# Moving the joining factors of the first head group into the gather loop, and starting GpSimd's decay arguments before them

## The reference, cut to what matters

```
S_t = diag(exp(log_g_t)) S_{t-1} + k_t^T v_t,     o_t = q_t S_t
```

## Time and profile before

| what | value |
|---|---|
| median of 3 runs | 2969.95 us (2969.85 to 2975.12) |
| profiled execution: its own time | 2969.85 us |
| profiled execution: span from first to last instruction | 2968.1 us |
| busy: PE, DVE, ACT, POOL | 82%, 71%, 38%, 28% of the span |
| `phase_scan` of layer 0 | about 206 to 344 us |
| `phase_scan` of layer 1 | about 2039 to 2128 us |

### The profile page before, as it was taken

The page is one execution under the profiler, slowest core; times in us unless marked ns, Lnnn a source line. Parts: engine busy times, 40 slices in busy tenths (PEclk is TensorE's granted clock), DMA queues, the critical chain, the costliest instruction groups (busy, mean ns, idle before and its releaser), DMA issues. The chain is left out here.

```text
span 2968.1 us, 36810 instructions
## 1 busy us (share of the span) xinstructions
PE 2424.4 (82%) x13114; PEld 1822.0 (61%) x13114; DVE 2110.2 (71%) x4654; ACT 1124.8 (38%) x2650; POOL 840.8 (28%) x688
## 2 busy tenths in 40 slices
PE   5979799896659888888888888688797897777776
PEld 3779565674659777777777777478556542223222
DVE  3567763499949888888888888667653898745444
ACT  3433354336633333333333333342344433334332
POOL 1004001230004434343433434103004453433431
PEclk8995799998889999999999999797798999999999
DMA  5210205264379999999999999221103999999997
GB/s 213 89 32 2 96 4 188 77 235 165 142 297 400 419 419 420 420 419 419 419 420 420 418 416 407 101 82 33 39 1 131 420 421 421 421 421 422 422 422 300
DMA packets 147671, 817.13 MB, mean 275 GB/s; under 512 B 16200, under 2 KB 17800, under 8 KB 64672
## 3 DMA queue, kind: packets, MB, share of 16 engines
q0 software_dynamic: 73728, 536.90, 43.7%
q1 hardware_dynamic: 73760, 277.87, 24.2%
HBM read 796.89 MB, written 17.83 MB: 274 GB/s over the span
## 5 line engine op out<-in xcount | busy, mean ns | idle before, releaser
L2412 POOL DMA_INDIRECT pair_ring<-in_uv_first,eid x256 | 395.0, 1543 | 780.9 <-DVE pair_sum L2555 274.5
L2051 PE MATMUL ps<-pair_ring,pair_diag 128*128 128x512 f32 x1024 | 475.4, 609 | 143.5 <-ACT pair_diag L2130 139.4
L2436 PE MATMUL ps<-peer_h,peer_uv 128*128 128x256 f32 x2048 | 474.8, 386 | 40.4 <-DMA peer_uv<-in_uv_dense 40.4
L2262 DVE CUSTOM_DVE_ANT_0 pair_ring<-pair_ring,hT 128x1024 f32<-128x1024 f32 x256 | 312.9, 1222 | 208.7 <-DMA pair_ring<-in_uv_rows,eid 208.6
L2051 PEld LDWEIGHTS ps<-pair_ring,pair_diag 128*128 128x128 f32 x1024 | 187.1, 192 | 421.0 <-ACT pair_diag L2130 222.6
L2436 PEld LDWEIGHTS ps<-peer_h,peer_uv 128*128 128x128 f32 x2048 | 387.3, 194 | 94.2 <-DMA peer_uv<-in_uv_dense 30.6
L119 PE MATMUL ps<-h_both 128*128 128x256 f32 x1024 | 316.0, 309 | 104.4 <-DVE h_both L2592 104.3
L2543 DVE CUSTOM_DVE_ANT_0 pair_ring<-pair_ring,hT 128x1024 f32<-128x1024 f32 x256 | 312.2, 1220 | 121.0 <-DMA pair_ring<-in_uv_first,eid 120.3
L2012 POOL DMA_INDIRECT pair_ring<-in_uv_rows,eid x256 | 270.4, 1056 | 397.9 <-PE ps L2051 360.2
L120 PE MATMUL ps<-h_both 128*128 128x256 f32 x1024 | 299.5, 292 | 0.0
L121 PE MATMUL ps<-h_both 128*128 128x256 f32 x1024 | 298.9, 292 | 0.0
(11 more groups left out here) (439 smaller groups left out, 4738.5 us busy)
## 6 DMA issues: line engine op xcount, KB each, us to landing
peer_uv<-in_uv_dense SPq DMA_DIRECT2D x128, 1024.0 KB
ada_slab<-in_ada_w SPq DMA_DIRECT2D x20, 2048.0 KB, 8.2
proj_slab<-in_w_fm SPq DMA_DIRECT2D x38, 512.0 KB, 3.5
route_slab<-in_w_pq SPq DMA_DIRECT2D x32, 512.0 KB
peer_gates<-dense_stage SPq DMA_DIRECT2D x4, 4096.0 KB, 13.1
peer_gates<-peer_gates SPq DMA_DIRECT2D x16, 1024.0 KB, 21.6
fm<-in_w_out SPq DMA_DIRECT2D x16, 512.0 KB, 4.2
fm<-in_ada_w SPq DMA_DIRECT2D x3, 2048.0 KB, 11.9
```

Of the source, the lines that this page charges most:

```text
L2051: mm = nc.tensor.matmul(ps[:, 4 + 2 * t + half, :], diag[:, s % DG, :], ring[:, s % R, D_MODEL + half * BANK:D_MODEL + (half + 1) * BANK], ...
L2262: nc.vector.tensor_tensor_reduce(out=row, in0=row, in1=hT[:, s // NS], scale=1.0, scalar=0.0, op0=ALU.mult, op1=ALU.add, accum_out=dots[:, ...
L2412: nc.gpsimd.indirect_dma_start(out=ring[:, s % R], out_offset=None, in_=d["uv_first"], in_offset=bass.IndirectOffsetOnAxis(ap=eid[:, s // ...
L2436: mm = nc.tensor.matmul(ps[:, e % 2, 0:n], us[:, e % SW, k, :], hw[:, k, :], start=(k == 0), stop=(k == DC - 1))
```

## The change

`joining_keys(0)` no longer stands before the gathers; it now runs inside the gather of pair 0, after unit 3, as it does for the other groups. GpSimd no longer waits for it, but for `ready` to reach 2, the end of both `level_keys(0, ...)`.

```diff
@@ -815,7 +815,7 @@
                         nc.gpsimd.memset(lk[:], 0.0).then_inc(zeroed, 1)
 
-                        pool.wait_ge(x_ready, 1)
+                        pool.wait_ge(ready, 2)
                         for dr in range(2):
                             query_arguments(nc.gpsimd, 1, dr)
                             key_arguments(nc.gpsimd, 1, dr).then_inc(pool_arg, 1)
@@ -884,7 +884,7 @@
                                 c = heads[2 * pr][0]
-                                if u == 3 and pr == first[c] and c:
+                                if u == 3 and pr == first[c]:
                                     joining_keys(c)
@@ -896,7 +896,6 @@
                         for dr in range(2):
                             level_keys(0, dr)
-                        joining_keys(0)
                         for pr in range(4):
                             gather(pr)
```

## The result

The median after is 2994.29 us (2992.89 to 2994.84, four runs) against 2969.90 us (2969.00 to 2975.12, four runs) for the kernel before: a ratio of 1.0077 with an interval of [1.0064, 1.009]. The prediction said 2977.7 us, in a range from 2969.5 to 2981.5. The direction was right, the size was wrong by a factor of three (24.4 us instead of 7.8).

What follows compares the result with a forecast made beforehand. TensorE paces layer 0's first pair; in layer 1 it runs nearly level with VectorE, which then sets the pace. Turns cost some 5.0 + 2.9 us, the middle 7.9, on 2969.85: 2977.7 us, range 2969.5 to 2981.5.

Steps and rivals of the forecast that it cites:

- They take turns, one for one, each waiting until the other is through.: Joining block beside GpSimd's subtractions: the engines alternate, costing 6.4 to 9.4 us in both layers together; chance 0.67.
- GpSimd's train wins: Rival: VectorE's joining block gets in only after GpSimd's 42 subtractions; 11.1 + 9.4 us, 2990.4 us; chance 0.09, wholly or in part.
- The length of the hold: Train rival's block times: layer 0 starts at 249.7, ends at 253.3 instead of 240.8; layer 1 ends at 2068.9, not 2059.4.
- The slack: Layer 0, pair 0: 1.4 us left between VectorE emptying unit 6 and TensorE needing its banks; none in layer 1.
- the gain of the move itself: Layer 1, pair 0: TensorE's 1.06 us stall moves to the pair's other end; second joining part gains 0.1 us.
- The price of a turn: Each wait of a joining-block instruction for one GpSimd subtraction costs 0.585 us in layer 0, 0.37 in layer 1.
- both bounds: Upper: one instruction per turn, 6.2 + 3.2 = 9.4 us; lower: two narrow ones per turn, 3.9 + 2.5 = 6.4 us.
- No price for copies out of PSUM: VectorE's copies beside GpSimd's subtractions keep their time: 1.69 us per unit with GpSimd busy, 1.70 without.
- GpSimd's earlier start costs nothing by itself: GpSimd starts at 225.1 instead of 228.75 and 2050.8 instead of 2053.32; nothing waits for ScalarE's earlier emptying.
- The clock: Rival: layer 1's removed gap raises TensorE's clock in pair 1, saving up to 5.8 us, perhaps 2967; chance 0.04 with other gains.

Runs made afterwards that it cites:

- pool_links: The changed kernel, but each of 36 of GpSimd's 42 subtractions is followed by a wait for its own result; 2976.24 us, ratio 1.001.
- pool_split: The changed kernel, but GpSimd waits for `x_ready` after its first 14 subtractions, before VectorE comes to the joining block; 2974.73 us against 2972.64, ratio 1.0002.
- pool_early_only: The kernel before with GpSimd's earlier start alone, the joining block left before the gathers; 2973.02 us against 2972.87, ratio 1.0.
- join_after_u2: The changed kernel with the joining block of c = 0 after unit 2 instead of unit 3, GpSimd's train of 42 unbroken; 2979.43 us against 2973.50.

## Why the prediction was wrong

**The step that failed** is the sentence "They take turns, one for one, each waiting until the other is through." It was read from `phase_out`, where every instruction of GpSimd waits on a semaphore first, and carried over to a train of 42 without a wait. `pool_links`, with a wait between the instructions, took turns; the same instructions without it didn't. In their place stands one wait for the rest of the train: 12.72 us in layer 0 and 8.27 in layer 1. The rival that had this, GpSimd's train wins, was dismissed on the same rows and got 0.09. It was priced at 11.1 + 9.4 = 20.5 us; the scans lost 11.9 + 9.6 = 21.5 us. That the direction came out right says nothing for the turns, since the train forecast the same direction.

**The length of the hold.** The rival had the block of layer 0 start at 249.7; on the clock of the kernel after, which runs 0.74 us later, that is 250.4, and it started in earnest at 250.5. In layer 1 it had the block behind the whole train; the hold broke in the fourth instruction from its end.

**The slack** of 1.4 us in layer 0 was sound, if a little small. In the kernel after the block grows by 12.72 - 0.28 = 12.44 us and the second joining part comes 10.68 later, so 1.8 us were absorbed. `pool_links` gives much the same: the block grows by 7.35 - 3.56 = 3.8, the joining part comes 43.95 - 41.86 = 2.1 us later, 1.7 absorbed. In layer 1 the gain of the move itself was 0.35 us, not 0.1: with the block undisturbed (`pool_split`) the second joining part starts at 23.80 us instead of 24.15.

**The price of a turn** was 0.585 us in the prediction, GpSimd's whole instruction, and 0.37 in layer 1. Where there are turns it is 0.42 to 0.43 in layer 0 (and 0.2 in layer 1, 0.49 instead of 0.28 us): 0.70 instead of 0.28 us for a narrow instruction, 0.85 instead of 0.42 for a wide one, 1.11 instead of 0.68 for the last. Part of GpSimd's instruction lies under VectorE's. One narrow instruction per turn is what unbroken trains show, two what `pool_links` shows; so both bounds had a case.

**No price for copies out of PSUM** held: 12 copies take 5.40 us behind the train, 5.44 beside it, and four beside it 1.69.

**GpSimd's earlier start costs nothing by itself** held (`pool_early_only`), and the prediction named the collision as what it would cost together with the move.

**The clock** had been a rival on the side of a gain. It went the other way, with the 1.5 us of the output of pair 0 in layer 0 and the 1.2 us of pairs 2 and 3 in layer 1; the removed gap in layer 1 did not raise it (112 instructions in 12.21 us in `pool_split`, 0.11 us each).

So with what the runs showed, the sum by the prediction's own steps is: layer 0, 12.4 - 1.7 = 10.7, and 1.5 for the clock, 12.2 (measured 11.9); layer 1, a hold of 8.0 and four turns of 0.2, less the 0.35 gained, 8.4 (measured 8.4), and 1.2 for the clock, 9.6 (measured 9.6). What stays open is the 3.3 us outside the scans, whether the count since GpSimd's last wait or the moment of arrival decides, and the reason for either.

## What to carry to other kernels

Before a two-input VectorE instruction on SBUF data is put beside GpSimd's work, count how many reading instructions GpSimd runs there without a wait: with a long unbroken train behind it the price was not a turn per instruction but the rest of the train, and the cheapest cure was a wait that GpSimd has to make before the block (`pool_split`), not a faster start. A price read from rows holds only for instructions that are linked as those in the rows are; check what each one waits for before carrying it over. When two parts of a change cover for each other, time each alone: here one was worth 0, the other +15.5 us, and together they lost more than either.

No version here beat the kernel before. In layer 0 the move has nothing to win, in layer 1 at most the 1.06 us that `pool_split` turned into other waits.

## What was not expected of the hardware

- A VectorE instruction of 0.28 us lasted 12.72 us beside 21 subtractions of GpSimd that each took their normal 0.585. The Trainium skill (SBUF — State Buffer, "SBUF: two separate sides") has the loser block for the whole instruction; here it blocked for a whole train of instructions. VectorE was let in up to the 14th instruction after GpSimd's last wait and held in the 16th and the 21st, with the moment of arrival as a rival that no run excludes.
- A wait that is met at once, visible only as 0.07 us on GpSimd, was worth 8 us of hold (12.72 against 4.64).
- The reverse holds too: VectorE's 13 instructions kept GpSimd out for 3.35 us.
- Once VectorE is in, it stays in: in `join_after_u2` it came in the 14th and took turns for all of its 13 instructions (0.50 to 1.11 us each), far beyond the 16th.
